# Modulation vectors of a hybrid decoder step: the column groups of TensorE split the output columns instead of the contraction

## The chip, the cores and the metric

The kernel runs on one core of one Trainium2 chip. The metric is the device time of one execution in microseconds; a lower figure is better. All arithmetic that this text speaks of is in float32.

## The reference, cut to what matters

One inference step of a two-layer trunk runs over 512 prompt tokens and 8 sample sequences of 8 tokens. Each of its four sub-layers (delta-rule mixer, mixture of experts, SSM mixer, mixture of experts) is modulated by a vector that depends on the sequence and not on the token:

```
def ada_mod(c, w_mod, b_mod):
    m = (jax.nn.silu(c) @ w_mod + b_mod)[:, None, :]
    shift, scale, gate = jnp.split(m, 3, axis=-1)
    return shift, scale, gate
...
        shift, scale, gate = ada_mod(c, w_mod_mix[i], b_mod_mix[i])
        hn = rmsnorm(x, norm_mix[i]) * (1.0 + scale) + shift
...
        x = x + gate * out
```

`c` has 9 rows (one prompt, 8 samples) of 1024, and each of the four `w_mod` is 1024 x 3072. So the modulation is four products of 9 x 1024 with 1024 x 3072, and their 48 MB of weights are read once. The change touches this product alone. The first mixer's input projection (1024 x 4112) runs on the same tokens in the same stretch of the program.

## The kernel before, in words

Everything lies transposed: 128 channels on the partitions, tokens on the columns. The engines are programmed separately and meet through semaphores.

**Modulation blocks.** The 3072 outputs of a sub-layer are cut into 6 blocks of 512, so there are 24 blocks `(m, nb)`. The weights of a block come in two ring units of 1 MB (`kh` = 0 and 1, four contraction chunks of 128 each), loaded by SyncE into a ring of 6 slots (`load`, L527). The silu of `c`, padded to 32 columns, is `c32`.
- `adaln(m, nb)` on TensorE (L870) makes 8 matmuls with a 128 x 32 stationary piece of `c32` and 512 moving weight columns. Contraction chunk `k` of a unit goes to the column group `32k:32k+32` of the array, so the four groups hold four partial sums of the same 512 outputs, on 4 x 32 partitions of PSUM.
- ScalarE copies this 128 x 512 block to SBUF (`modulation` on ScalarE, L1546): for the first four blocks into a place each in `big`, for the 20 others (`LATE`) all into the one place `rb[:, 0:512]`; it waits there until the turn of the block before has read it.
- `adaln_turn(m, nb)` (L882) makes 4 matmuls with 128 columns of that block as stationary operand and a 128 x 9 selection matrix (`cst[:, MISC, 48:57]`) as moving one. They add the four partial sums and turn the block, so that outputs lie on partitions and the 9 sequences on columns.
- VectorE adds the bias into `modT` (`modulation` on VectorE, L1848); after a sub-layer's block 3 it also forms 1 + scale times the norm's weight (L1853, L1854).

**Order.** The first four blocks (shift and scale of the first sub-layer) run at the start of the program, before anything can be projected: the input `hT` is made from them by ScalarE (L1555). The 20 others are laid between the 32 output blocks `m` of the input projection (`project`, L829). In round `m` TensorE does, in this order:

```
            for m in range(32):
...
                project(f"p{m}", w[:, m % 2], hT)
...
                if 2 <= m < 18:
...
                if 1 <= m <= N_LATE:
                    adaln_turn(*LATE[m - 1])
                if m < N_LATE:
                    adaln(*LATE[m])
```

The omitted middle for 2 <= m < 18 is a sum of squares for the l2 norm of q and k (L1342). VectorE's part of round `m` is the bias of late block `m - 2` (L1848), the short convolution of `p{m}` (L1979 to L1985), and a reciprocal and a product for the l2 norm of block `m - 3` (L1993, L1994). ScalarE copies `p{m}` out of PSUM (L1591), applies silu (L1608), squares (L1614) and takes a root (L1622), and then copies the modulation block. PSUM is used as four buffers in turn (`begin`): a buffer may be filled again when its reader of four uses ago has reported, so a turn waits until VectorE has read the turn of the round before.

Elsewhere in the program, `from_state` (L1043) and the sum `osum` (L1363) let the four column groups work beside each other, with 128 and 144 moving columns and 32 stationary ones, and `tile_sums` (L848) adds eight full-width products of 128 columns into the same PSUM columns.

A matmul of the code leaves two records of a weight load and two of a matmul in the trace (24 blocks of 8 matmuls in L870 give 384 records).

Of the kernel before, what the change touches and what calls it, by code (L numbers as in the profile page):

```python
# [139 lines left out]
def trunk(nc, d, o, book):  # L140
    units = ring_units()
    unit_no = {u: n for n, u in enumerate(units)}
    with ExitStack() as ctx:
# [45 lines left out]

        m_sb = [big[:, 512 * nb:512 * nb + 512] for nb in range(4)] + [rb[:, 0:512]]  # L190
        c32 = zT[:, :, :].rearrange("p k t -> p (k t)")[:, 0:KD * 32].rearrange("p (k c) -> p k c", c=32)
# [612 lines left out]
        def _(pe):  # L804
# [58 lines left out]
            def adaln(m, nb):  # L863

                ps = begin(f"ada{m}_{nb}")
                for kh in range(2):
                    n = unit_no["mod", m, 2 * nb + kh]
                    w = weights(n).rearrange("p (k c) -> p k c", k=4)
                    for k in range(4):
                        mm = pe.matmul(ps[32 * k:32 * k + 32, 0, :], c32[:, 4 * kh + k, :], w[:, k, :],  # L870
                                       start=(kh == 0), stop=(kh == 1), skip_group_check=True)
                    book["unit_read", n] = state["n"]
                mm.then_inc(acc_full, 1)

            def adaln_turn(m, nb):

                pe.wait_ge(act_drained, at(f"read:ada{m}_{nb}"))
                out = flatbuf(f"adaT{m}_{nb}", 4, 9)
                begin(f"adaT{m}_{nb}")
                src = m_sb[4 if (m, nb) in LATE else nb]  # L880
                for j in range(4):
                    mm = pe.matmul(out[:, j, :], src[:, P * j:P * j + P], cst[:, MISC, 48:57],  # L882
                                   start=True, stop=True, skip_group_check=True)
                mm.then_inc(acc_full, 1)

# [526 lines left out]
        def _(act):  # L1412
# [127 lines left out]
            def modulation(m, nb):  # L1540
                act.wait_ge(acc_full, filled(f"ada{m}_{nb}"))
                late = (m, nb) in LATE
                if late and (m, nb) != LATE[0]:

                    act.wait_ge(acc_full, filled("adaT%d_%d" % LATE[LATE.index((m, nb)) - 1]))
                act.activation(m_sb[4 if late else nb], buf(f"ada{m}_{nb}")[:, 0, :], ACT.Copy).then_inc(  # L1546
                    act_drained, up(act_drained, f"read:ada{m}_{nb}"))
# [224 lines left out]
        def _(dve):  # L1772
# [73 lines left out]
            def modulation(m, nb):  # L1846
                dve.wait_ge(acc_full, filled(f"adaT{m}_{nb}"))
                tt(modT[:, m, 4 * nb:4 * nb + 4], flatbuf(f"adaT{m}_{nb}", 4, 9),  # L1848
                   bc(bmod[:, m, 4 * nb:4 * nb + 4], 2, 9), ALU.add).then_inc(
# [816 lines left out]
```

## Time and profile before

| | |
|---|---|
| median of 3 runs | 1509.86 us (1507.49 to 1511.36) |
| the profiled execution, its own time | 1505.48 us |
| its span, first to last instruction | 1503.8 us |
| busy TensorE (matmul) | 1310.9 us, 87% |
| busy VectorE, ScalarE, GpSimd | 43%, 24%, 10% |
| mean granted TensorE clock | 0.92 |
| L870, the modulation's matmuls | 48.1 us busy, 384 records |
| L882, the turn's matmuls | 192 records of 257 ns |

A record of a matmul lasts longer than its share of the engine, because matmuls are pipelined: 384 records of about 0.6 us in L870 occupy 48.1 us together. So what a piece costs is read here from the time between two starts, not from durations. The granted clock is given as a share of 2.4 GHz: 1.00 is 2.4 GHz, 0.50 is 1.2 GHz.

### The profile page before, as it was taken

Reading aid. Unit: us, or ns where it says so; the run is one execution under the profiler, and the core shown is the slowest. Engines: PE = TensorE matmul, PEld = TensorE weight load, DVE = VectorE, ACT = ScalarE, POOL = GpSimd, SP = SyncE. Lnnn points to the kernel's source line nnn. Section 1 sums busy time; section 2 is a strip of 40 time slices with the busy share of each in tenths; the row PEclk is TensorE's granted clock in tenths of the full one; section 3 lists DMA queues with packets and bytes.
Section 4 is the critical chain, followed back from the end, with each engine's and each line's share of the span. In section 5 each row is a group of like instructions: output and inputs, shape, how many; then the busy total and the mean of one; then the engine's idle time right before and its main releaser. Section 6 shows DMA issues by size and latency. Waiting matters only on the chain.

```text
span 1503.8 us, 20584 instructions
## 1 busy us (share of the span) xinstructions
PE 1310.9 (87%) x8254; PEld 1046.3 (70%) x8254; DVE 639.8 (43%) x1120; ACT 359.7 (24%) x451; POOL 144.3 (10%) x268
## 2 busy tenths in 40 slices
PE   5999999999989899739999759989999549999854
PEld 3676777777789877527788647887777438887644
DVE  3657776686633434511111169875111601111106
ACT  3445544243111300401111044201000501111003
POOL 0112111210000000075000020000000020000011
PEclk9999999999989989859999969969999869999986
DMA  8546456782111521549999481696411059999824
GB/s 348 213 204 280 194 227 257 299 334 60 42 41 43 163 56 57 196 168 375 382 358 349 168 293 48 102 195 188 177 62 58 27 212 351 348 352 355 300 89 150
DMA packets 113483, 305.37 MB, mean 203 GB/s; under 512 B 40512, under 2 KB 66880, under 8 KB 89600
## 3 DMA queue, kind: packets, MB, share of 16 engines
q1 hardware_dynamic: 107728, 282.31, 53.3%
q0 software_dynamic: 5680, 22.02, 4.1%
q8 instruction: 52, 0.85, 0.2%
q14 instruction: 23, 0.19, 0.0%
HBM read 241.07 MB, written 63.23 MB: 202 GB/s over the span
## 4 chain that ended last, share of the span: by engine, by line
PE 49%; DVE 6%; DMA 5%; issue 2%; SPq 2%; ACT 2%; POOL 1%; POOLq 0%; DVEq 0%; ACTq 0%
PE acc L1137 16%; PE acc L829 10%; PE acc L1145 8%; PE acc L1393 4%; PE acc L1295 2%; DMA yT<-xs 1%; POOL xs L2503 1%; PE acc L839 1%; DVE rb L1789 1%; PE acc L848 1%; DMA s_y<-big 1%; PE acc L1091 1%; DVE zT L2248 1%; DMA big<-ys,row_of 1%; ACT zT L1481 1%
## 5 line engine op out<-in xcount | busy, mean ns | idle before, releaser
L829 PE MATMUL acc<-hT,ring 128*128 128x288 f32 x1280 | 320.4, 410 | 7.7 <-DVE hT L1800 7.7
L829 PEld LDWEIGHTS acc<-hT,ring 128*128 128x128 f32 x1280 | 242.2, 191 | 92.0 <-issue 27.3
L1137 PEld LDWEIGHTS acc<-zT,ring 128*128 128x128 f32 x2176 | 253.3, 195 | 20.4 <-issue 14.3
L1137 PE MATMUL acc<-zT,ring 128*128 128x128 f32 x2176 | 254.1, 279 | 4.6 <-ACT zT L1476 2.3
L1145 PE MATMUL acc<-ring,zT 128*128 128x512 f32 x272 | 124.9, 602 | 8.6 <-DVE zT L2248 2.9
L2248 DVE TENSOR_TENSOR zT<-zT,acc 128x256 f32<-128x256 f32 x32 | 13.5, 421 | 249.8 <-ACT zT L1481 249.8
L1145 PEld LDWEIGHTS acc<-ring,zT 128*128 128x128 f32 x272 | 48.9, 189 | 64.4 <-issue 62.2
L829 PE MATMUL acc<-yT,ring 128*128 128x288 f32 x384 | 93.3, 406 | 0.0
L2253 DVE COPY yT<-acc 128x1024 f32<-128x1024 f32 x32 | 39.2, 1224 | 124.8 <-PE acc L1145 124.8
L1481 ACT ACTIVATE zT<-acc 128x256 f32<-128x256 f32 x32 | 12.3, 385 | 316.9 <-PE acc L1137 316.9
L829 PEld LDWEIGHTS acc<-yT,ring 128*128 128x128 f32 x384 | 73.0, 190 | 20.2
L1128 PE MATMUL acc<-cst,yT 128*128 128x128 f32 x272 | 37.9, 286 | 52.8 <-DMA yT<-xs 52.8
L1128 PEld LDWEIGHTS acc<-cst,yT 128*128 128x128 f32 x272 | 32.8, 148 | 54.3 <-issue 50.2
L1393 PE MATMUL acc<-yT,ring 128*128 128x288 f32 x256 | 65.0, 416 | 0.2 <-issue 0.2
L1993 DVE RECIPROCAL yT<-yT 128x576 f32<-128x576 f32 x16 | 60.0, 3753 | 0.6
L1393 PEld LDWEIGHTS acc<-yT,ring 128*128 128x128 f32 x256 | 49.5, 195 | 14.6 <-issue 0.6
L1981 DVE SCALAR_TENSOR_TENSOR big<-yT,extra,big 128x512 f32<-128x512 f32 x72 | 54.1, 752 | 2.6
L2503 POOL DMA_INDIRECT xs<-big,row_of x20 | 19.1, 956 | 358.7 <-DVE row_of L2226 353.3
L2427 DVE TENSOR_TENSOR hT<-acc,extra 128x576 f32<-128x576 f32 x8 | 6.1, 758 | 110.9 <-ACT extra L1761 110.9
L870 PE MATMUL acc<-ring,zT 128*32 128x512 f32 x384 | 48.1, 618 | 1.7 <-DMA ring<-in_w_mod_mix 1.7
L1201 PE MATMUL acc<-cst,big 128*128 128x128 f32 (+1 forms) x80 | 15.6, 362 | 37.5 <-DVE big L2285 37.4
L1591 ACT ACTIVATE yT<-acc 128x576 f32<-128x576 f32 x24 | 15.6, 651 | 124.6 <-PE acc L829 119.4
(408 smaller groups left out, 1684.8 us busy)
## 6 DMA issues: line engine op xcount, KB each, us to landing
ring<-in_w SPq DMA_DIRECT2D x102, 1024.0 KB, 8.3
ring<-in_w_mod_mix SPq DMA_DIRECT2D x24, 1024.0 KB, 10.2
ring<-in_w_mod_ffn SPq DMA_DIRECT2D x24, 1024.0 KB, 8.0
yT<-xs SPq DMA_DIRECT2D x34, 512.0 KB, 8.7
ring<-in_w_in SPq DMA_DIRECT2D x16, 1024.0 KB, 10.8
ys<-yT SPq DMA_DIRECT2D x32, 512.0 KB, 8.2
xs<-S SPq DMA_DIRECT2D x3, 4096.0 KB, 33.2
ring<-in_glu SPq DMA_DIRECT2D x8, 1024.0 KB, 8.7
```

The costliest lines, as they stand in the source:

```text
L829: mm = pe.matmul(ps[:, b, 0:HT], w[:, k, :], rhs[:, k, HT * b:HT * b + HT], start=(k == 0), stop=(k == KD - 1))
L870: mm = pe.matmul(ps[32 * k:32 * k + 32, 0, :], c32[:, 4 * kh + k, :], w[:, k, :], start=(kh == 0), stop=(kh == 1), skip_group_check=True)
L1128: mm = pe.transpose(xt[:, k, :], x[:, P * k:P * (k + 1)], cst[:, IDENT, :])
L1137: mm = pe.matmul(acc[:, H_ACC, x, P * f:P * (f + 1)], wv[:, f, k, :], xt[:, k, :], start=(k == 0), stop=(k == KD - 1), skip_group_check=True)
L1145: mm = pe.matmul(y[:, b, :], hd[:, P * f:P * (f + 1)], w2[:, D * f + 512 * b:D * f + 512 * (b + 1)], start=(f == 0), stop=(f == 1))
L1295: mm = pe.matmul(ps[:, b, 0:HT], w[:, x, k, :], yT[:, k, HT * b:HT * b + HT], start=(k == 0), stop=(k == KD - 1))
L1393: mm = pe.matmul(ps[:, b, 0:HT], w[:, m % 2, k, :], yT[:, k, HT * b:HT * b + HT], start=(k == 0), stop=(k == KD - 1))
L1981: step(stt(dst, raw[m % 2][:, j:j + SEQ], cw[:, m, j:j + 1], dst, ALU.mult, ALU.add))
L1993: step(dve.reciprocal(ln[(m - 3) % 2], ln[(m - 3) % 2]))
L2248: tt(hid[j], s1[j], acc[:, H_ACC, 1, 0:2 * P], ALU.mult).then_inc(hid_ready, 1)
L2253: dve.tensor_copy(yc[j], acc[:, Y_ACC + j].rearrange("p b c -> p (b c)")).then_inc(yc_ready, 1)
L2503: pool.indirect_dma_start(xs[:, :], bass.IndirectOffsetOnAxis(ap=row_of[0:n, k, t:t + 1], axis=0), htok[t][0:n, :], None).then_inc(scatter ...
```

## The change

The four column groups no longer share out the contraction but the outputs. Group `g` takes outputs `128g` to `128g+127` of the block and runs over all 8 contraction chunks; each chunk is now 4 matmuls of 128 moving columns, one for each group, with the same stationary piece of `c32`. A block is 32 matmuls instead of 8, and no partial sums are left: PSUM holds 128 x 128 finished values (group on the partitions' upper bits, sequence on the lower ones). ScalarE copies 128 columns instead of 512. One matmul with the identity as moving operand turns the block; VectorE reads the 9 of each 32 columns with a step. The late blocks get two places in `rb` in turn, so a copy waits for the turn of two blocks before.

```
-        m_sb = [big[:, 512 * nb:512 * nb + 512] for nb in range(4)] + [rb[:, 0:512]]
+        m_sb = [big[:, P * nb:P * nb + P] for nb in range(4)] + [rb[:, P * i:P * i + P] for i in range(2)]
+
+        def mod_block(m, nb):
+
+            return m_sb[4 + LATE.index((m, nb)) % 2 if (m, nb) in LATE else nb]
...
                     for k in range(4):
-                        mm = pe.matmul(ps[32 * k:32 * k + 32, 0, :], c32[:, 4 * kh + k, :], w[:, k, :],
-                                       start=(kh == 0), stop=(kh == 1), skip_group_check=True)
+                        for g in range(4):
+                            mm = pe.matmul(ps[B * g:B * g + B, 0, 0:P], c32[:, 4 * kh + k, :], w[:, k, P * g:P * g + P],
+                                           start=(kh == 0 and k == 0), stop=(kh == 1 and k == 3),
+                                           skip_group_check=True)
...
                 pe.wait_ge(act_drained, at(f"read:ada{m}_{nb}"))
-                out = flatbuf(f"adaT{m}_{nb}", 4, 9)
-                begin(f"adaT{m}_{nb}")
-                src = m_sb[4 if (m, nb) in LATE else nb]
-                for j in range(4):
-                    mm = pe.matmul(out[:, j, :], src[:, P * j:P * j + P], cst[:, MISC, 48:57],
-                                   start=True, stop=True, skip_group_check=True)
-                mm.then_inc(acc_full, 1)
+                ps = begin(f"adaT{m}_{nb}")
+                pe.matmul(ps[:, 0, 0:P], mod_block(m, nb), cst[:, IDENT, :], start=True, stop=True).then_inc(acc_full, 1)
...
-                late = (m, nb) in LATE
-                if late and (m, nb) != LATE[0]:
-
-                    act.wait_ge(acc_full, filled("adaT%d_%d" % LATE[LATE.index((m, nb)) - 1]))
-                act.activation(m_sb[4 if late else nb], buf(f"ada{m}_{nb}")[:, 0, :], ACT.Copy).then_inc(
+                late = LATE.index((m, nb)) if (m, nb) in LATE else 0
+                if late > 1:
+
+                    act.wait_ge(acc_full, filled("adaT%d_%d" % LATE[late - 2]))
+                act.activation(mod_block(m, nb), buf(f"ada{m}_{nb}")[:, 0, 0:P], ACT.Copy).then_inc(
...
-                tt(modT[:, m, 4 * nb:4 * nb + 4], flatbuf(f"adaT{m}_{nb}", 4, 9),
+                tt(modT[:, m, 4 * nb:4 * nb + 4], flatbuf(f"adaT{m}_{nb}", 4, B)[:, :, 0:9],
```

On TensorE the rounds 2 and 3 of the projection read before, from the projection of round 2 on (L829 the projection, L1342 the sum of squares, L882 the turn, L870 the block):

```order
L829 MATMUL acc<-hT,ring 128x288 x16
L1342 MATMUL acc<-yT,ones 128x288 x2
L882 MATMUL acc<-cst,rb 128x9 x4
L870 MATMUL acc<-ring,zT 32x512 x8
L829 MATMUL acc<-hT,ring 128x288 x16
L1342 MATMUL acc<-yT,ones 128x288 x2
L882 MATMUL acc<-cst,rb 128x9 x4
L870 MATMUL acc<-ring,zT 32x512 x8
```

Nothing moves between its neighbours; the same place of TensorE after the change (L834 the projection, L886 the turn, L876 the block):

```order
L834 MATMUL acc<-hT,ring 128x288 x16
L1344 MATMUL acc<-yT,ones 128x288 x2
L886 MATMUL acc<-cst,rb 128x128
L876 MATMUL acc<-ring,zT 32x128 x32
L834 MATMUL acc<-hT,ring 128x288 x16
L1344 MATMUL acc<-yT,ones 128x288 x2
L886 MATMUL acc<-cst,rb 128x128
L876 MATMUL acc<-ring,zT 32x128 x32
```

Four turning matmuls of 9 columns became one of 128, and eight matmuls of 512 columns became 32 of 128.

At the start of the program TensorE runs the first four blocks and their turns in this order before the change (L839 is the norm's sum, L1091 the first reader of `hT`):

```order
L839 MATMUL acc<-yT,ones 128x288 x16
L870 MATMUL acc<-ring,zT 32x512 x16
L882 MATMUL acc<-cst,big 128x9 x4
L870 MATMUL acc<-ring,zT 32x512 x8
L882 MATMUL acc<-cst,big 128x9 x4
L870 MATMUL acc<-ring,zT 32x512 x8
L882 MATMUL acc<-cst,big 128x9 x8
L1091 MATMUL acc<-hT,w_ba 32x288 x14
```

and the same rows of TensorE after it:

```order
L844 MATMUL acc<-yT,ones 128x288 x16
L876 MATMUL acc<-ring,zT 32x128 x64
L886 MATMUL acc<-cst,big 128x128
L876 MATMUL acc<-ring,zT 32x128 x32
L886 MATMUL acc<-cst,big 128x128
L876 MATMUL acc<-ring,zT 32x128 x32
L886 MATMUL acc<-cst,big 128x128 x2
L1093 MATMUL acc<-hT,w_ba 32x288 x14
```

Here too the order is kept, and the last two turns still stand together ahead of the first reader of `hT`.

## Rows read from the trace of the kernel before

**Rows 1.** The page: busy time of TensorE and its granted clock in 40 slices
```profile
PE   5999999999989899739999759989999549999854
...
PEclk9999999999989989859999969969999869999986
```

**Rows 2.** Busy time by stretch: us, engines (records), granted clock, DMA share, GB/s
```profile
57.00:285.50 228.50, 228.50 (x1196) 162.46 (x1196) 156.18 (x228) 107.67 (x130) 39.52 (x80) 1.00 0.56 227
28.20:35.00 6.80, 5.89 (x27) 2.92 (x27) 6.50 (x2) 1.67 (x4) 0.00 (x0) 0.50 1.03 406
35.00:41.80 6.80, 4.71 (x39) 2.84 (x38) 4.25 (x9) 1.62 (x4) 0.00 (x0) 1.00 1.02 419
41.80:45.20 3.40, 2.59 (x16) 2.15 (x18) 2.85 (x15) 3.40 (x6) 0.00 (x0) 0.50 1.01 419
```

**Rows 3.** TensorE in time order, one projection round: start us, us, records
```profile
136.99 1.92 PE L870 MATMUL acc<-ring,zT 128*32 128x512 f32 x16
...
146.71 1.13 PE L1342 MATMUL acc<-yT,ones 128*128 128x288 f32 x4
147.68 0.95 PE L882 MATMUL acc<-cst,rb 128*128 128x9 f32 x8
148.57 1.92 PE L870 MATMUL acc<-ring,zT 128*32 128x512 f32 x16
150.42 0.75 PE L829 MATMUL acc<-hT,ring 128*128 128x288 f32 x2
```

**Rows 4.** TensorE in time order where a full-width stage meets L1043
```profile
513.26 1.39 PE L1038 MATMUL acc<-yT,big 64*128 64x128 f32 x11
514.58 3.70 PE L1043 MATMUL acc<-big,extra 128*32 128x128 f32 x128
```

**Rows 5.** Durations of a record, ns min/median/max, for L870, L1043 and L848
```profile
L870 PE MATMUL acc<-ring,zT x384: 592/592/1062, 20.8 to 275.3; 128*32 128x512 f32 x192
...
L1043 PE MATMUL acc<-big,extra x128: 272/273/297, 514.6 to 518.0; 128*32 128x128 f32 x128
...
L848 PE MATMUL acc<-zT,ones x34: 275/275/377, 885.5 to 890.0; 128*128 128x128 f32 x34
```

**Rows 6.** TensorE in time order where products add into the same columns
```profile
524.50 4.07 PE L1363 MATMUL acc<-yT,cst 128*32 128x144 f32 x64 [1.41 <-ACT yT L1688]
...
887.99 5.57 PE L848 MATMUL acc<-zT,ones 128*128 128x128 f32 x48
```

**Rows 7.** Waits from 57 to 302 us: us in total, times, longest
```profile
ACT yT L1591 <- PE acc L829: 116.2, 21, 9.5
DVE big L1979 <- ACT yT L1591: 64.6, 20, 8.5
ACT rb L1546 <- PE acc L870: 1.3, 1, 1.3
```

**Rows 8.** VectorE in time order around round 18
```profile
263.45 0.50 DVE L1979 TENSOR_SCALAR big<-yT,extra 128x512 f32<-128x512 f32 x1 [2.65 <-ACT yT L1591]
...
272.18 0.20 DVE L1848 TENSOR_TENSOR modT<-acc,bmod 128x36 f32<-128x36 f32 x1
...
274.05 0.50 DVE L1979 TENSOR_SCALAR big<-yT,extra 128x512 f32<-128x512 f32 x1 [1.18 <-ACT yT L1591]
```

**Rows 9.** TensorE's matmuls and weight loads (PEld) in time order, round 18
```profile
263.33 1.92 PE L870 MATMUL acc<-ring,zT 128*32 128x512 f32 x16
265.18 8.03 PE L829 MATMUL acc<-hT,ring 128*128 128x288 f32 x32
273.05 0.95 PE L882 MATMUL acc<-cst,rb 128*128 128x9 f32 x8
...
272.81 1.10 PEld L882 LDWEIGHTS acc<-cst,rb 128*128 128x128 f32 x8
```

**Rows 10.** Weight loads issued from 57 to 286 us, and SyncE's issues in one round
```profile
DMA to landing us min/median/max: 4.7/8.8/13.0
...
135.33 3.97 SPq L527 DMA_DIRECT2D ring<-in_w_mod_mix  x4
```

**Rows 11.** The end of the stretch: VectorE's row masks, and TensorE's first use of them
```profile
299.90 1.23 DVE L1927 TENSOR_TENSOR yT<-cst,gt 128x1024 f32<-128x1024 f32 x1
...
302.27 1.88 PE L894 MATMUL acc<-yT,ones 128*128 128x512 f32 x4
```

**Rows 12.** TensorE in time order at the start of the program
```profile
37.16 1.06 PE L870 MATMUL acc<-ring,zT 128*32 128x512 f32 x8 [0.40 <-DMA ring<-in_w_mod_mix]
38.15 1.95 PE L882 MATMUL acc<-cst,big 128*128 128x9 f32 x16
42.61 0.78 PE L1091 MATMUL acc<-hT,w_ba 128*32 128x288 f32 x2 [2.50 <-ACT hT L1555]
```

**Rows 13.** ScalarE and VectorE in time order between these, and a ScalarE copy of 256 columns
```profile
38.35 0.60 ACT L1546 ACTIVATE big<-acc 128x512 f32<-128x512 f32 x1 [3.10 <-PE acc L870]
...
40.21 0.20 DVE L1848 TENSOR_TENSOR modT<-acc,bmod 128x36 f32<-128x36 f32 x1 [0.70 <-PE acc L882]
...
40.68 0.23 DVE L1854 TENSOR_TENSOR modA<-modA,nrm 128x72 f32<-128x72 f32 x1
...
41.03 1.52 ACT L1555 ACTIVATE hT<-yT,modT,modA 128x512 f32<-128x512 f32 x2 [2.08 <-DVE modA L1854]
...
L1481 ACT ACTIVATE zT<-acc x32: 384/385/386, 675.7 to 1412.7; 128x256 f32<-128x256 f32 x32
```

## The prediction
> **What bounds the kernel now.** I read the page first. TensorE is busy 9 tenths or more in nearly all of the slices that hold the input projection, at the full granted clock [rows 1]. The busy times by stretch then say it sharply: from 57 to 285.5 us, where 20 of the 24 modulation blocks lie, TensorE is busy 228.50 of 228.50 us at clock 1.00 (2.4 GHz), while VectorE has 156 us of work and ScalarE 108 [rows 2]. The waits agree: ScalarE stood 116 us waiting for TensorE's projection and VectorE 65 us for ScalarE's copy of it [rows 7]. So in this stretch whatever TensorE saves is saved from the time, until another engine or a load is late. Before 57 us it is otherwise: TensorE waits for a weight unit to land and, at 42.61, 2.50 us for `hT` [rows 12], so there the chain from the last weight unit through ScalarE and VectorE to `hT` counts.
>
> The third view is TensorE in time order over one round [rows 3]. A reader should look at the starts alone: the turn starts at 147.68, the block at 148.57, the next projection at 150.42. A turn thus takes 0.89 us of the engine and a block 1.85 us. Together this is 2.74 us in a round of 148.57 - 136.99 = 11.58.
>
> **The turn.** Removed are 4 matmuls (8 records), added is one (2 records). What is left is one step between two full-width records of 128 columns, and the passage from such a record to a column-group matmul. Rows of the same shapes give both. Forty-eight records of L848 take 5.57 us [rows 6], the last lasts 0.275 [rows 5], so a step is (5.57 - 0.275) / 47 = 0.11 us. L1038 ends at 513.26 + 1.39 = 514.65, its last record began about 0.27 earlier at 514.38, and L1043, which works on 32-column groups, starts at 514.58 [rows 4]: the passage is 0.20 us. The new turn takes 0.11 + 0.20 = 0.31 us and saves 0.89 - 0.31 = **0.58 us**. It is not a quarter of the old one, because the passage stays. Round 20's turn is followed by a projection and not by a block; I price it the same.
>
> **The block.** The 16 records of 512 columns become 64 of 128. The nearest row is L1043 [rows 4]: 128 records of just this shape, 128 moving columns on 32 stationary ones, the four groups in turn, at the same full clock. They take 3.70 us; without the last record's 0.27 [rows 5] the first and the last start 3.43 us apart, which for 32 sets of four is 3.43 / 31 = 0.11 us a set. A block is 16 sets: 15 x 0.11 = 1.65 us to the last set, and 0.02 within it. Before, the last record began 1.92 - 0.59 = 1.33 us after the first [rows 3, 5], and the projection 0.07 us before that record's end (148.57 + 1.92 = 150.49 against 150.42). With the same lead the new block hands over 0.27 - 0.07 = 0.20 us after its last record starts: 1.65 + 0.02 + 0.20 = 1.87 us. The block costs **0.02 us more** than before, so it is no gain by itself: four groups over 512 columns in 4 sets, or over 128 columns in 16 sets, stream the same number of columns.
>
> One thing differs from L1043: successive sets add into the same PSUM columns, 0.11 us apart, while a record lasts 0.27. Two rows show such sums without a stall. L848 adds its products into the same columns every 0.11 us [rows 6]. L1363 does it on the column groups: 64 records, 16 sets of 144 columns in 4.07 us, about 0.24 us a set, which is what 0.11 us becomes at half clock with 144 columns instead of 128 (0.11 x 2 x 144 / 128 = 0.25). So I take 0.11 us. The lower end of the block's price is what it costs now, 1.85 us, since the column stream is the same; the upper end is in the first rival.
>
> Twenty late rounds save 20 x (0.58 - 0.02) = **11.2 us**.
>
> **What is late next in these rounds.** The weight loads: SyncE issues four units at 135.33, and the round's block, their first user, starts at 148.57 [rows 10, 3], 13.2 us later. The median landing is 8.8 us after issue and the longest of the stretch 13.0 [rows 10], and the issues move with TensorE since each waits for a freed slot. A saving of 0.6 us in the 13.2 leaves the first unit some 12.6 us; it is the first of its four in the queue. No block waited for a load in the stretch. I cost it at nothing. VectorE: in an ordinary round it idles 2.65 us before the convolution [rows 8], so it stays covered. Round 18 has no sum of squares, and there the idle time is 1.18 us. Its turn needs the PSUM buffer that VectorE's L1848 frees at 272.18 + 0.20 = 272.38 [rows 8]; the turn's first weight load stands at 272.81 [rows 9]. From VectorE's end to the start of an engine that waits for it I take 0.12 us (L1854 ends at 40.68 + 0.23 = 40.91, ScalarE's L1555 starts at 41.03 [rows 13]). So the margin is 0.31 us; the round shrinks by 0.56, so TensorE will wait about **0.25 us** once. At the stretch's end, VectorE's first row mask is done at 299.90 + 1.23 = 301.13, and TensorE's first use of it starts at 302.27 [rows 11]. That margin of 1.1 us loses only round 20's 0.58, since VectorE's chain itself starts from projection 20. It holds.
>
> ScalarE's copy shrinks from 0.60 us to an estimated 0.28 (the 256-column copy takes 0.385 [rows 13], so 256 columns are worth 0.215 and 128 some 0.11 less than that copy). In the late rounds it lies beside a whole projection, and so does the second place in `rb`, which takes away a wait of which 1.3 us in one case is all that the row of ScalarE's copy shows, and that was for the block's matmuls [rows 7]. Both are worth nothing there. VectorE's read with a step of 32 has the same 36 elements: nothing.
>
> **The first four blocks.** The last weight unit is what starts the chain, at 37.16 [rows 12], and it lands no sooner. Its half block takes 1.06 us now, and 7 x 0.11 + 0.02 + 0.27 = 1.06 after, so ScalarE's copy starts at 38.35 as before and ends at 38.63 instead of 38.95. Now both last turns take 1.95 us in one row from 38.15, and the bias follows at 40.21, 0.37 us after the last record began (38.15 + 1.95 - 0.26 = 39.84). After the change the first of them is done before the copy is. The last starts at 38.63 + 0.12 = 38.75, its second record at 38.86, and the bias at 39.25: **0.95 us** earlier, and `hT` with it, for which TensorE waits. The granted clock changes between 0.50 and 1.00 here [rows 2]; if it falls elsewhere, one or two us may come or go, which goes into the range.
>
> **Sum.** -11.2 + 0.25 - 0.95 = -11.9 us. On the profiled execution's 1505.48 us that is 1493.6. Against the median of the runs shown, 1509.86 (4.4 us above that execution), it is **1498.0 us**, 0.8% faster. About 0.3%, some 4.5 us, is what a measurement of this kernel tells from no change. Nothing after 286 us has a reason to give the time back: what follows starts from projections and loads that all move with TensorE.
>
> **Rival 1, slower: the records set the pace, not the columns.** A block has 64 records instead of 16. If each needed its own 0.11 us, the step of full-width records of 128 columns [rows 6], the block would take 64 x 0.11 = 7.0 us, 5.2 us more, and 20 rounds would give 1498 + 104 = 1602 us; the point from which it decides is a block of 2.43 us, 0.038 us a record. Against it: L1043's 128 records start within 3.43 us, 0.027 us a record [rows 4]. For it: L1043 is one short burst of 3.7 us, and here TensorE takes 20 of them between other work. Chance 0.05. The Trainium skill has a rule that points this way: in "TensorE: Matmul & The Clock Gate" (section on 56 ns against 53.3 ns) it says that without hardware decoding the sequencer spends about 62 ns on each matmul. By that page a block would take an estimated 64 x 0.062 = 4.0 us and the program some 1540 us. The trace speaks against it, with 27 ns a record in the row of L1043.
>
> **Rival 2, no change: another wait takes the saved time.** VectorE or a weight load becomes the end of every round, as I expect for round 18 alone. VectorE's own work of 8.9 us (11.58 less 2.65 idle [rows 8]) in a round of 11.0 speaks against it; for it speaks only that its margin in round 18 is as small as 0.3 us. If all 11.2 us were lost, 1508.9 us remain; if half, 1503.6. Chance 0.08, most of it within 0.3%.
>
> **How the numbers follow.** The forecast, with the durations above, has 0.87. Its bounds: a passage between 0.11 and 0.30 us moves the sum by 2 us either way, the clock at the start by 1 to 2, the median of a few runs by 2. So 1493 to 1503 holds most of it; I let the range reach to 1503.5 for the half-lost case. Faster by over 0.3%: 0.88 (the forecast and a little of rival 2). Within 0.3%: 0.07. Slower: 0.05, rival 1.
>
> **What the changed profile would show.** Turn to block 0.31 us and block to projection 1.87 us in the time order of a round; L876's busy time near 47 us with 1536 records; no wait of TensorE for VectorE but a short one in round 18; L1557, the first `hT`, near 40.1 us; the stretch of 20 rounds 11 us shorter. A block above 2.43 us, or TensorE idle in every round, would prove me wrong.

## The result

The change is faster by more than forecast. The median is 1488.04 us (1485.72 to 1492.54, 5 runs) against 1511.36 us (1507.49 to 1512.27, 5 runs) of the kernel before: a ratio of 0.9853, interval 0.9835 to 0.9871. The forecast was 1498.0 us with a range from 1493.0 to 1503.5. The sign was right, and in the stretch that was changed the mechanism too; the size was not, and the time lies 5 us below the range. One execution of a later experiment (e4 below) took 2574 us at a mean granted clock of 0.841, for no reason that the runs show; it is left out of every figure.

### The profile after

The page of the changed kernel. TensorE has 1008 matmul records and 1008 weight loads more than before (8254 of each there), L876 is busy for 49.4 us where some 47 were expected, and the instruction queue q8 fetched 60 pieces (52 before):

```profile
PE 1298.3 (87%) x9262; PEld 1062.0 (71%) x9262; DVE 639.8 (43%) x1120; ACT 351.9 (24%) x451; POOL 145.7 (10%) x268
...
PEclk9899999999899899769999869969999869999986
...
q8 instruction: 60, 0.98, 0.3%
...
L876 PE MATMUL acc<-ring,zT 128*32 128x128 f32 x1536 | 49.4, 282 | 3.3 <-DMA ring<-in_w_mod_mix 3.3
```

TensorE in time order over one round of the changed kernel (start us, us, records), to be laid beside [rows 3]:

```profile
132.24 0.38 PE L886 MATMUL acc<-cst,rb 128*128 128x128 f32 x2
132.56 1.95 PE L876 MATMUL acc<-ring,zT 128*32 128x128 f32 x64
134.44 8.03 PE L834 MATMUL acc<-hT,ring 128*128 128x288 f32 x32
...
143.28 0.39 PE L886 MATMUL acc<-cst,rb 128*128 128x128 f32 x2
```

From turn to block are 0.32 us, from block to projection 1.88 us, and the round takes 143.28 - 132.24 = 11.04 us. The forecast said 0.31, 1.87 and 11.58 - 0.56 = 11.02.

VectorE's bias and TensorE's weight load of the turn in round 18 of the changed kernel, the place of the small margin [rows 8, 9]:

```profile
262.36 0.20 DVE L1850 TENSOR_TENSOR modT<-acc,bmod 128x36 f32<-128x36 f32 x1
```
```profile
262.45 0.43 PEld L886 LDWEIGHTS acc<-cst,rb 128*128 128x128 f32 x2
```

The load starts before the bias ends at 262.56, so it is not held back by it. The matmul that writes the buffer starts at 262.69, 7.86 us after its projection (254.83), as the turn of round 17 does (252.63 after 244.77): it did not wait either. From turn to turn round 18 takes 10.06 us and took 10.61 (262.44 to 273.05), so TensorE lost nothing there.

The start of the changed kernel in time order, TensorE and then ScalarE, beside [rows 12, 13]:

```profile
36.27 1.94 PE L876 MATMUL acc<-ring,zT 128*32 128x128 f32 x32 [1.33 <-DMA ring<-in_w_mod_mix]
38.13 1.32 PE L886 MATMUL acc<-cst,big 128*128 128x128 f32 x4
41.97 5.43 PE L1093 MATMUL acc<-hT,w_ba 128*32 128x288 f32 x32 [2.51 <-ACT hT L1557]
```
```profile
40.38 5.75 ACT L1557 ACTIVATE hT<-yT,modT,modA 128x512 f32<-128x512 f32 x8 [1.77 <-DVE modA L1856]
```

`hT` starts at 40.38 us, 0.65 earlier than in the trace of before. All this is near the forecast, and the two profiled executions, 1505.48 and 1492.54 us, are 12.9 us apart, though the medians are 23.3. But the 12.9 us are not the forecast's 11.9. Where the projection goes on behind the last turn, the change leads by 286.67 - 276.87 = 9.80 us (only the starts count here):

```profile
286.67 15.77 PE L829 MATMUL acc<-hT,ring 128*128 128x288 f32 x64
```
```profile
276.87 9.38 PE L834 MATMUL acc<-hT,ring 128*128 128x288 f32 x38
```

The rest came where the prediction did not look, at the first matmuls of the gdn stage behind the projection (the delta-rule mixer). TensorE in time order there, of the kernel before and then of the change:

```profile
407.85 3.68 PE L860 MATMUL acc<-ring,yT 128*128 128x64 f32 x16 [3.24 <-DMA ring<-gdn_m]
411.32 1.91 PE L916 MATMUL acc<-cst,big 128*128 128x128 f32 x8
```
```profile
396.11 2.39 PE L865 MATMUL acc<-ring,yT 128*128 128x64 f32 x16 [1.37 <-DMA ring<-gdn_m]
398.29 1.92 PE L918 MATMUL acc<-cst,big 128*128 128x128 f32 x8
```

TensorE waited 3.24 us for a reload of `gdn_m`, and now waits 1.37; the 16 records behind the wait are shorter too. At the next row the lead is 411.32 - 398.29 = 13.03 us, some 3 us more than ahead of the stage, and it is 13.0 us at the end of the span. Nothing of this stage was changed. That the two profiled executions differ by about what was forecast is luck: 9.8 us of the change's steps and 3.2 us of something else.

### The profile page after: what moved, and what is told of

It is laid out like the page before. It is cut to its first block and busy times, and to the rows that moved or that the text cites. A ratio compares the mean times of both kernels' runs of the same rounds, so it can differ in the third digit from the quotient of the medians.

```text
span 1490.8 us, 22600 instructions
## 1 busy us (share of the span) xinstructions
PE 1298.3 (87%) x9262; PEld 1062.0 (71%) x9262; DVE 639.8 (43%) x1120; ACT 351.9 (24%) x451; POOL 145.7 (10%) x268
## 5 line engine op out<-in xcount | busy, mean ns | idle before, releaser
L834 PE MATMUL acc<-hT,ring 128*128 128x288 f32 x1280 | 322.0, 412 | 7.7 <-DVE hT L1802 7.7
L834 PEld LDWEIGHTS acc<-hT,ring 128*128 128x128 f32 x1280 | 243.6, 192 | 80.1 <-issue 15.2
L834 PE MATMUL acc<-yT,ring 128*128 128x288 f32 x384 | 93.3, 406 | 0.0
L834 PEld LDWEIGHTS acc<-yT,ring 128*128 128x128 f32 x384 | 73.1, 190 | 20.0
L1483 ACT ACTIVATE zT<-acc 128x256 f32<-128x256 f32 x32 | 12.3, 384 | 316.4 <-PE acc L1139 316.4
L876 PE MATMUL acc<-ring,zT 128*32 128x128 f32 x1536 | 49.4, 282 | 3.3 <-DMA ring<-in_w_mod_mix 3.3
L876 PEld LDWEIGHTS acc<-ring,zT 128*32 128x32 f32 x1536 | 41.7, 113 | 7.5 <-DMA ring<-in_w_mod_mix 3.3
## 6 DMA issues: line engine op xcount, KB each, us to landing
ring<-in_w_in SPq DMA_DIRECT2D x16, 1024.0 KB, 12.5
```

The source lines that it names most:

```text
L834: mm = pe.matmul(ps[:, b, 0:HT], w[:, k, :], rhs[:, k, HT * b:HT * b + HT], start=(k == 0), stop=(k == KD - 1))
L876: mm = pe.matmul(ps[B * g:B * g + B, 0, 0:P], c32[:, 4 * kh + k, :], w[:, k, P * g:P * g + P], start=(kh == 0 and k == 0), stop=(kh == 1 a ...
```

## Experiments

All runs in one table: median of n runs, ratio to the kernel before on the same chip, mean time at half clock (2 x (1 - mean granted clock) x span, from each run's own figures), and the wait for `gdn_m` in the profiled execution. The first run of the change had 233 us at half clock, the kernel before 248 to 253 in its six sets. The ratio is an estimate of its own and not that of the two medians: e16 is 2.5 us faster than its kernel before by medians and 5.0 by its ratio.

| run | median us (n) | ratio, interval | half clock us | wait for gdn_m us |
|---|---|---|---|---|
| e1 before again | 1508.63 (12) | 1.0006, 0.9984 to 1.0028 | 251 | 3.04 |
| e2 change again | 1489.47 (6) | 0.9875, 0.9846 to 0.9905 | 238 | 1.15 |
| e3 turn of four | 1513.28 (12) | 1.0032, 1.0007 to 1.0056 | 259 | 2.94 |
| e4 one place | 1486.06 (5) | 0.9847, 0.9819 to 0.9875 | 223 | 1.13 |
| e5 change + 23 | 1504.97 (12) | 0.9974, 0.9951 to 0.9998 | 246 | 1.14 |
| e6 change + 2 | 1495.05 (6) | 0.9914, 0.9891 to 0.9938 | 244 | 1.22 |
| e7 change + 4 | 1494.99 (12) | 0.9911, 0.9888 to 0.9934 | 246 | 1.34 |
| e8 before + 23 | 1515.19 (11) | 1.0059, 1.0039 to 1.0079 | 242 | 1.16 |
| e9 change, gaps filled | 1485.42 (6) | 0.9836, 0.9806 to 0.9866 | 217 | 1.14 |
| e10 before, gaps filled | 1499.52 (8) | 0.9937, 0.9910 to 0.9964 | 218 | 3.07 |
| e11 one place, gaps filled | 1484.28 (5) | 0.9843, 0.9818 to 0.9868 | 215 | 1.25 |
| e12 as e9, again | 1486.98 (5) | 0.9843, 0.9814 to 0.9871 | 215 | 1.22 |
| e13 before, 16 at the start | 1504.68 (12) | 0.9984, 0.9964 to 1.0004 | 243 | 1.14 |
| e14 change, 8 at the start | 1496.29 (6) | 0.9922, 0.9896 to 0.9947 | 247 | 3.16 |
| e15 change, 24 at the start | 1493.15 (6) | 0.9904, 0.9876 to 0.9931 | 247 | 1.24 |
| e16 before, 56 at the start | 1505.19 (12) | 0.9967, 0.9944 to 0.9990 | 241 | 1.32 |
| e17 before, 64 at the start | 1509.09 (12) | 1.0004, 0.9980 to 1.0028 | 248 | 2.89 |
| e18 change, 64 at the start | 1492.71 (6) | 0.9891, 0.9849 to 0.9932 | 243 | 1.14 |

### Both kernels again, and the turn by itself

e1 and e2 are the two kernels unchanged.

> The kernel before, unchanged, timed against itself, with the granted clock of each execution. Theory A (the change is worth the 12 us of its own steps, and the rest of the 22 us between the medians is spread between executions): ratio 1.000, but single executions spread by 6 us or more, and the profiled one of before (1505.48) lies inside that spread. Theory B (the changed timing also shortens stages after 290 us, in most executions): ratio 1.000 and executions between 1507 and 1513 us, so that 1505.48 was a rare one.

> The changed kernel, unchanged. Theory A: median within 1493 to 1501 us on a second occasion, ratio near 0.992. Theory B: the ratio stays at 0.983 to 0.987, the executions at 1484 to 1493 us, and the faster ones have a mean granted clock above 0.92, that is less time at half clock after 290 us.

The gain is there again, some 19 us (1508.6 against 1489.5). e1's executions spread over 13 us with 1505.48 among them, as theory A said; e2's median lies below A's 1493 to 1501, and its ratio of 0.9875 at the edge of B's. Neither theory has both.

e3 keeps the new block and takes back the turn's form, four matmuls instead of one:

```
-                ps = begin(f"adaT{m}_{nb}")
-                pe.matmul(ps[:, 0, 0:P], mod_block(m, nb), cst[:, IDENT, :], start=True, stop=True).then_inc(acc_full, 1)
+                out = flatbuf(f"adaT{m}_{nb}", 4, 9)
+                begin(f"adaT{m}_{nb}")
+                for j in range(4):
+                    mm = pe.matmul(out[:, j, :], mod_block(m, nb), cst[:, IDENT, B * j:B * j + 9],
+                                   start=True, stop=True, skip_group_check=True)
+                mm.then_inc(acc_full, 1)
```

> The changed kernel with the turn made of four matmuls of 9 columns again (one for each column group); the block, the copies and the two places stay as changed. Both theories: turn to block 0.89 us instead of 0.31, block 1.88 us, so 20 x 0.58 = 11.6 us more up to 290 us than the changed kernel, and the stage up to there as in the kernel before. Theory A: the whole time returns to within 3 us of the kernel before (ratio 0.998 to 1.002). Theory B: if what shortens the later stages hangs on the block's shape, the ratio is near 0.993; if it hangs on when the later stages begin, 1.000.

TensorE in time order over the end of one round of e3:

```profile
138.43 0.95 PE L888 MATMUL acc<-cst,rb 128*128 128x9 f32 x8
139.31 1.95 PE L876 MATMUL acc<-ring,zT 128*32 128x128 f32 x64
141.20 5.12 PE L834 MATMUL acc<-hT,ring 128*128 128x288 f32 x20
```

The turn takes 0.88 us again and the block 1.89. The whole gain is gone: it hangs on the turn, as the prediction had it, and the new block is worth nothing by itself. e3 is even some 5 us slower than the kernel before, with an interval above 1; its 259 us at half clock against 250 go along with that, but nothing here explains it. By this run the surplus, too, hangs on the turn, which is odd for something that lies 100 us later.

e4 takes away the second place in `rb`, so that each copy waits for the turn of the block before:

```
-            return m_sb[4 + LATE.index((m, nb)) % 2 if (m, nb) in LATE else nb]
+            return m_sb[4 if (m, nb) in LATE else nb]
...
-                if late > 1:
+                if late > 0:
...
-                    act.wait_ge(acc_full, filled("adaT%d_%d" % LATE[late - 2]))
+                    act.wait_ge(acc_full, filled("adaT%d_%d" % LATE[late - 1]))
```

> The changed kernel with one place for all late blocks again, so that a copy waits for the turn of the block before. Both theories: the turn of the block before is done a whole projection earlier, so the wait costs nothing and the time is that of the changed kernel within 2 us. A rival (the second place is what pays the part of the gain that was not forecast): some 10 us more than the changed kernel.

The second place is worth nothing, as forecast; with one place the median is even 3 us lower than in e2, with intervals that overlap.

### The first theory: clock in later stages

Within the runs of the kernel before, time and half-clock time go together: over 113 executions in six sets a microsecond more at half clock goes with 0.34 us more time (correlation 0.91). The first theory (S, where the expectations use a letter) was that the surplus is time at half clock in later stages, which depends on when these start; its rival (N), that the later stages do not depend on it, so that an inserted delay adds just itself. e5 to e8 insert a delay in round 20, ahead of the last turn: 23 matmuls of 0.49 us (11.2 us) in both kernels, and 2 or 4 in the change.

```
+                    for _ in range(23 if (m, nb) == LATE[-1] else 0):
+                        pe.matmul(ps[:, 1, 0:HT], ones[:, :], hT[:, 0, 0:HT], start=True, stop=True, skip_group_check=True)
```

> The changed kernel with 23 extra matmuls of 288 columns (0.485 us each, 11.2 us together, into unused PSUM columns) on TensorE in round 20, ahead of the last turn, so that everything after the 20 rounds starts about as late as in the kernel before. Theory S (the part of the gain that was not forecast comes from the later stages, whose time at half clock depends on when they begin): the time returns to that of the kernel before, 1505 to 1511 us, with about 250 us at half clock. Theory N (the later stages are quicker for a reason that stays with the changed kernel): 1489 + 11.2 = 1500 us, with about 235 us at half clock.

> The same with 2 extra matmuls, 0.97 us. Theory S: the time moves by more than 3 us, up or down, and the time at half clock moves with it by 5 us or more. Theory N: 1490 us, the time at half clock stays at 235.

> The same with 4 extra matmuls, 1.94 us. Theory S: again a step of several us against the changed kernel, not the one of 2 extra matmuls. Theory N: 1491 us.

> The kernel before with the same 23 extra matmuls in round 20. Theory S: not 1508 + 11.2 = 1519 us, but some us off it, with the time at half clock off its 250 us. Theory N: 1519 us within 2, half clock 250 us.

11.2 us inserted into the change cost 15.5 us, 0.97 us cost 5.6, 1.94 us cost 5.5 (against e2), while 11.2 us in the kernel before cost only 7. By medians the later stages answer to a small edit before them, with an answer that does not grow with the delay. Theory N fits none of the four medians, but it is not refuted: the ratio intervals of e6 and e7 overlap that of e2, and e8's ratio allows 5.9 to 11.9 us. S has half an explanation at most, since the extra half-clock time of e6 (6 us more than e2) accounts for 2 us of its 4.6 us surplus. The four edits also add 8, 16 and 92 records ahead of the later stages, and e8 with its 92 has a wait for `gdn_m` of 1.16 us and not 3: the second theory below makes some 3 us of its missing 4 out of that.

e9 and e10 hold the clock up in one later stage, the SSM mixer's answers, by filling three gaps in which TensorE waits for VectorE; e11 and e12 do so with one and with two places.

```
+                    for _ in range({0: 13, 1: 15, 7: 8}.get(k, 0)):
+                        pe.matmul(ps[:, 0, 4 * NCK:4 * NCK + P], ones[:, :], ones[:, :], start=False, stop=False,
+                                  skip_group_check=True)
                     pe.wait_ge(entry_states_ready, at(f"sin{k}"))
```

> The change, with TensorE given 13, 15 and 8 extra matmuls (128 columns, into PSUM columns that nobody reads) in the three gaps of the SSM mixer's answers in which it waits for VectorE's entry states (3.11, 3.52 and 1.93 us idle before L1272 in the second run of the change, with 24 us at 1.2 GHz in the stage). If what is left over of the gain is time at half clock in later stages, TensorE stays at 2.4 GHz here in every execution: the stage from the first to the last L1272 takes some 43 to 46 us and not 50.2, half-clock time falls by 15 to 25 us, and the time by 4 to 8 us against the change, to 1482 to 1486 us, with less spread. If half-clock time has no price of its own (it only goes along with the time), the extra matmuls do nothing or cost up to 1 us: 1488 to 1491 us.

> The kernel before with the same extra matmuls in the same three gaps. If half-clock time in this stage is one of the things in which the two kernels differ by chance of their start, both now spend the same time in it, and the difference between the two filled kernels is nearer the -12 to -13.5 us of the change's own steps than the -19.5 us between the unfilled ones: this one 1497 to 1502 us, the other some 13 to 16 us below it. If the change's surplus comes from elsewhere, the difference stays at 19 to 20 us.

> The change with one place in rb for the late blocks and with the three filled gaps. With two places the one place was some 3 us faster. If that was the clock of the SSM answers falling out well in its executions (22 us there instead of 27 in its trace), the filled gaps take that advantage away, and what is left is at most the 1.7 us of the stretch at 1.2 GHz near 268 us that its trace does not show: 1483 to 1486 us, at most 2 us below the filled change of the same job. If one place has a gain of its own, it adds to the filled gaps': 1480 to 1483 us, 3 us or more below.

> The change with the three filled gaps, unchanged, on the same chip as the version with one place: 1483 to 1488 us, as before, a ratio of 0.982 to 0.986.

TensorE in time order there, in e2 and then in e9:

```profile
963.35 2.00 PE L1264 MATMUL acc<-yT,ring 128*128 128x72 f32 x16
968.46 3.69 PE L1272 MATMUL acc<-zT,big 64*128 64x72 f32 x32 [3.11 <-DVE zT L2394]
```
```profile
963.86 2.01 PE L1264 MATMUL acc<-yT,ring 128*128 128x72 f32 x16
965.71 3.11 PE L1267 MATMUL acc<-ones 128*128 128x128 f32 x26
968.95 2.01 PE L1275 MATMUL acc<-zT,big 64*128 64x72 f32 x32
```

Filled, the same 32 records take 2.01 us and not 3.69. The kernel before gains 10.6 us by medians; the change gains 2 to 4 us against e2, with ratio intervals that overlap. Both then have the same time at half clock (217 and 218 us). Still they are 1499.52 - 1485.42 = 14.1 us apart, of the 19 between e1 and e2. So some 5 us of the difference went with the clock in this stage, as expected, and 14.1 us are still more than the forecast steps of the change. By the spread of the executions this difference is uncertain by some 2 us. The one place of e4 brings nothing clear beside that (1484.28 against 1486.98, ratios alike): its 3 us were clock too, or chance.

### The second theory: an instruction fetch in the way of a store

Why the 3.24 us wait? The DMA view of the kernel before from 399.5 to 405.6 us, from the issue of two stores to the first reload that waits for them (queue, packets, MB; then the issues, KB each and median us from issue to landing):

```profile
q8 instruction: 1, 0.02, 1.0%
issues: line engine op xcount, KB each, median us to landing
gdn_m<-ring SPq DMA_DIRECT2D x1, 512.0 KB, 3.3
gdn_n<-ring SPq DMA_DIRECT2D x1, 512.0 KB, 5.5
```

The same view of the change from 389.6 to 393.8 us, without a row for q8:

```profile
q1 hardware_dynamic: 288, 1.05, 62.5%
issues: line engine op xcount, KB each, median us to landing
gdn_m<-ring SPq DMA_DIRECT2D x1, 512.0 KB, 2.6
gdn_n<-ring SPq DMA_DIRECT2D x1, 512.0 KB, 3.5
```

In the kernel before, one instruction fetch of 16 KB (0.85 MB in 52 fetches) falls between the stores, the second of which lands 5.5 us after issue and not 3.5. The reloads wait for both stores and are issued when the second has landed; SyncE in the kernel before and then in the change (the second store was issued at 400.05 and 390.16):

```profile
405.54 0.81 SPq L630 DMA_DIRECT2D ring<-gdn_m  x2
```
```profile
393.73 0.81 SPq L635 DMA_DIRECT2D ring<-gdn_m  x2
```

Where in the program a fetch falls depends on how many instructions stand before it. The change adds 2016 records to TensorE's program ahead of this stage. From before to e3 the program grows by 2 x (9406 - 8254) = 2304 records and 9 fetches, 256 records a fetch; the change's 2016 are 7 x 256 + 224. So in the change the fetches lie elsewhere, in e3 where they lay before, and e3 has the wait of 2.94 us. The Trainium skill states the 256 instructions of a fetch in "Runtime: NRT & Kernel Launch" (section on instruction fetch mechanics), which agrees; it also calls the cost of crossing such a boundary mostly hidden, and here one is not.

That gives an experiment which changes nothing but the lie of the fetches: a few small matmuls at the start of the program, where TensorE waits for over 8 us (24 of them took 0.83 us), each of four records.

```
                 ps = begin(f"ssq{i}")
                 src = yT if i == 0 else zT
+                for e in range(16 if i == 0 else 0):
+                    pe.matmul(ps[32 * (e % 4):32 * (e % 4) + 32, 0, HT:HT + 8], ones[:, 0:32], ones[:, 0:8],
+                              start=True, stop=True, skip_group_check=True)
```

e13 has 16 of them in the kernel before, e14 and e15 have 8 and 24 in the change (2016 + 32 is 8 fetches exactly; the expectation of e14 says 9, which is a slip).

> The kernel before with 16 extra matmuls of 8 columns at its start, where TensorE waits for ScalarE until 11.35 us, so that they cost nothing by themselves. They move each later instruction fetch of TensorE 64 records (some 8 us) earlier in its program. If the fetch of 16 KB at 402 us, between the issue of the gdn_m and gdn_n stores (399.66) and their landing (405.5), is what makes the stores slow, then they land some 3.5 us after issue and not 5.5, TensorE waits 1.2 us for gdn_m and not 3.24, and the time falls by 2 us, and by more (up to 6 us, to 1502 to 1506 us) where the clock then falls later too. If the fetch only happens to lie there, the wait stays above 3 us and the time at 1507 to 1510 us.

> The change with 8 such extra matmuls at its start: TensorE's records before the gdn stage are then a whole number of fetches (9 x 256) more than in the kernel before, so the fetch falls into the gdn stores again, as in the kernel before. If the fetch carries the surplus of the gain, the stores land some 5.5 us after issue, TensorE waits 3.1 us for gdn_m, and the time is 1491 to 1496 us, some 14 us below the kernel before. If not, 1487 to 1491 us and a wait of 1.2 us.

> The change with 24 extra matmuls at its start, the control for the extra matmuls' own cost: the fetches lie as in the kernel before with 16 extra ones, outside the stores. By the theory of the fetch: a wait of 1.2 us for gdn_m and 1485 to 1491 us, below the version with 8. If extra matmuls at the start cost time by themselves: above it.

TensorE at the gdn stage's first matmul, and the DMA view of the stores, in e13 (401.5 to 405.7 us) and then in e14 (388 to 394.2 us):

```profile
407.81 2.00 PE L863 MATMUL acc<-ring,yT 128*128 128x64 f32 x16 [1.14 <-DMA ring<-gdn_m]
```
```profile
gdn_n<-ring SPq DMA_DIRECT2D x1, 512.0 KB, 3.6
```
```profile
396.30 3.68 PE L868 MATMUL acc<-ring,yT 128*128 128x64 f32 x16 [3.16 <-DMA ring<-gdn_m]
```
```profile
q8 instruction: 1, 0.02, 1.0%
...
gdn_n<-ring SPq DMA_DIRECT2D x1, 512.0 KB, 5.5
```

The cause of the wait is shown in both directions: taken out of the kernel before, the fetch no longer delays the store; put into the change, it does. In all 20 traces of the table and of the two kernels the wait is 2.89 us or more where no record or a whole number of fetches was added ahead of this stage, and 1.37 us or less elsewhere; in each of these six traces, and in no other, a fetch stands in the DMA view of the stores, which land after 5.3 to 5.5 us and not 3.5 to 3.6. In time e13 gains 3.0 us by medians, its interval just reaching 1.0004; e14 is 3.1 us slower than e15. But e15 is also 3.7 us slower than e2, which the theory did not say. Three more runs were to tell whether the fetches carry that too: e16 gives the kernel before the lie of the change (56 extra matmuls, 224 records), e17 and e18 shift both kernels by one whole fetch (64).

> The kernel before with 56 extra matmuls of 8 columns at its start (24 took 0.83 us there, in a wait of TensorE of over 8 us). They put 224 records ahead of all others: with that, TensorE's fetches lie at the same instructions of its later stages as in the change, whose 2016 extra records are 7 x 256 + 224. If the surplus of the change is the lie of its fetches, this kernel is some 12 us slower than the change and not 20: 1500 to 1502 us, 6 to 8 us faster than the kernel before, without one instruction of the change. If not: 1505 to 1509 us, the 2 to 3 us of the fetch that no longer falls into the gdn stores at most.

> The kernel before with 64 extra matmuls, 256 records, one whole fetch: the control. The fetches lie where they lay, the wait for gdn_m is 3.0 to 3.3 us again, and the time 1506 to 1510 us, as the kernel before. If extra matmuls at the start are worth or cost something by themselves, it shows here.

> The change with 64 extra matmuls, one whole fetch: the control for the change. By the theory of the fetches the wait for gdn_m is 1.2 to 1.4 us and the time 1487 to 1491 us, as the change itself, and below the versions with 8 and 24 extra matmuls (1496 and 1493 us). If these were slower because of extra matmuls at the start, this one is slower still: 1495 us or more.

e17 is the kernel before again, in time and in its wait, so extra matmuls at the start cost that kernel nothing. e16 is 2.5 us faster by medians than the kernel before, with an interval below 1: less than the 6 to 8 us that were expected if the whole surplus followed the lie, though its ratio (1.5 to 8.4 us) does not exclude them. e18 should have been the change itself and came out 3.2 us above e2, though their intervals overlap; e14, e15 and e18 all lie above e2, so that a cost of the extra matmuls in the change is not excluded.

What the pairs with the same lie agree on is the change itself:

| lie of the fetches | before | change | difference of medians |
|---|---|---|---|
| in the stores | 1507.71 (timed beside e14) | 1496.29 (e14) | -11.4 |
| 64 records earlier | 1504.68 (e13) | 1493.15 (e15) | -11.5 |
| the change's own | 1505.19 (e16) | 1492.71 (e18) | -12.5 |

For the first pair the interval is that of e14's ratio, 0.9896 to 0.9947, or -15.7 to -8.0 us; by the spread of their executions the other two differences are uncertain by some 5 us each.

## Why the prediction was right, and where not

**The turn and the block: right.** 0.32 and 1.88 us stand against 0.31 and 1.87, both taken from other lines of the trace of before with the same shapes. A round lost 0.54 us, 20 rounds 10.8 (forecast 11.2, less 0.25 in round 18).

**Rival 1: refuted.** 64 records in 1.88 us are 0.029 us each. The 62 ns of the Trainium skill ("TensorE: Matmul & The Clock Gate", section on 56 ns against 53.3 ns) would have made the block an estimated 4.0 us; no run here shows that price.

**Rival 2 and the wait in round 18: neither came.** The margin was counted to the turn's weight load, which the trace of the change shows not to wait for VectorE; what writes the buffer is the matmul, 0.24 us later. So it was 273.05 - 272.50 = 0.55 us [rows 8, 9], just what the round lost, and 0.25 us of the sum were not there.

**The start: right in kind, too small.** `hT` starts at 40.0 us on average in the six traces of the change and of e4 to e7, and at 41.8 in those of before, e1 and e8: some 1.8 us earlier and not 0.95. Over all traces but e3 it is 39.9 us against 42.4, so 2.5. The last turns of the kernel before took 1.95 us in its first trace, at granted clock 1.00, and 3.59 in e1, at 0.50; those of the change took 1.32 in its first trace, at 0.50, and 1.01 in e14, at 1.00. The forecast had priced both at full clock. (By its own terms it should have had the bias at 38.86 + 0.37 = 39.23 and not 39.25, a slip of 0.02 us.)

**The clock inside a full stretch: not foreseen.** From the 8-column matmuls of L1317 on, most traces of the change hold a stretch at 1.2 GHz that no trace of the kernel before has. The stretch's row, and the projection in the change and then in e4, where it is missing:

```profile
267.80:271.30 3.50, 3.50 (x9) 2.44 (x8) 0.21 (x2) 0.00 (x0) 0.00 (x0) 0.51 1.01 419
```
```profile
267.10 9.72 PE L834 MATMUL acc<-hT,ring 128*128 128x288 f32 x32
```
```profile
267.44 8.03 PE L834 MATMUL acc<-hT,ring 128*128 128x288 f32 x32
```

It costs 1.7 us and stands in 8 of the 12 traces of the change's versions (without e3). With it the steps are worth 10.8 + 1.8 - 1.7 = 10.9 us, without it 12.6, or 0.7 more with the start of all traces: the pairs of equal lie measured 11.4 to 12.5. The traces say the same without any median. The projection behind the last turn starts at 286.7 to 289.1 us, 288.4 on average, in the six traces of the kernel before that have nothing inserted in round 20, and at 274.9 to 277.2, 276.1 on average, in nine of the change's versions: 12.3 us. So **the sum of -11.9 us was about the worth of the change's own steps**, in part by luck: the start gave some 1.5 us more than its term, and the stretch at 1.2 GHz, which has no term, took back 1.1 to 1.3 on average.

**The step that failed** is the sentence that nothing after 286 us has a reason to give the time back, since all that follows moves with TensorE. It put the later stages at nothing, looked for a loss alone, and was not true: in the two profiled executions the lead grows from 9.8 to 13.0 us in the gdn stage. Instruction fetches after 286 us do not move with TensorE's time but with the number of records, and the time at half clock differs between versions whose later stages are the same code. Of the 19 us between e1 and e2 (23 in the first measurement) 11.4 to 12.5 are the change's steps. Some 2.5 to 3.0 us are the fetch that no longer falls into the gdn stores (e13 and e16, by medians; by their ratios 2.4 and 5.0, and only e16's interval lies below 1). The remaining 4 us, or 8 by the first measurement, go along with time at half clock, 233 and 238 us in the two sets of the change against 243 to 247 in e14, e15 and e18, and 10 us of that go with some 3 us by the slope above. That is a correlation and not a cause shown. e9 and e10 speak for the clock of the SSM answers: with those gaps filled the kernels are 14.1 us apart, and since e10 has the fetch in its stores and e9 has not, the change's steps and the fetch (13.9 to 15.5 us) leave nothing over within its 2 us. Why the change, without extra matmuls, has less of it than e18 is open, and since e2 and e18 overlap, part of it may be chance.

**The range** was too narrow for the same reason. It allowed 2 us for the passage, 1 to 2 for the clock at the start and 2 for the median, and nothing for later stages, though edits that have no work in those (e6, e7, e18) moved the medians by 3 to 5 us.

## What to carry to other kernels

Price a matmul edit from the steps between starts of the same shapes elsewhere in the trace; that held here to 0.01 us for either piece. Count the records that an edit adds or takes away as well: on a long unrolled program they shift every later instruction fetch, and a store or reload that TensorE waits for can gain or lose 2 us with no edit near it. To learn what an edit itself is worth, compare it with a kernel before whose fetches lie alike, by a few small matmuls in an idle place, and leave some 5 us of a kernel like this to the clock in later stages.

## What the runs showed of the hardware that was not expected

- One instruction fetch of 16 KB beside two stores of 512 KB: the second lands 5.5 us after issue and not 3.5, though the fetch took 1.0% of 16 engines' time in 6.1 us, 1 us of one engine. Some 400 GB/s run in the body of the stores and then, for 1.6 us, 27 GB/s at most, about a sixteenth, as the view of the kernel before over the 40 slices of 399.5 to 405.6 us shows:

```profile
GB/s 0 0 0 0 0 0 269 376 403 430 430 403 376 376 349 376 403 403 430 510 376 376 349 135 0 27 0 0 27 0 27 27 27 27 27 27 0 0 0 0
```

The trace's own list of DMA packets, which the views only sum, shows the order. The fetch is one packet of 16 KB from 402.49 us, 0.95 us long. All but eight of the stores' 4 KB packets have started by 403.1; the eight run one behind the other from 403.42, when the fetch ends, to 405.05. In e14 four run so from 392.56 to 393.56, behind a fetch that ends at 392.57. That is what one DMA engine would do that took the fetch ahead of its share of the stores; the list does not name the engines, so this much is argued.

- The granted clock can fall to 1.2 GHz while TensorE has no gap at all, right behind 0.11 us steps of 8-column matmuls (267.8 us above). The same steps without the fall stand in 4 of the 12 traces of the change's versions and in all seven of the kernel before, so they alone do not decide it, and what does is open.
- Filling 8 us of waits with matmuls that compute nothing made the kernel before faster, by 10.6 us by medians (ratio 0.9937, 0.9910 to 0.9964). e9, e11 and e12 were the fastest versions by medians beside e4, but their ratios (0.9836 to 0.9843) are not told apart from those of the change (0.9853 and 0.9875).
